# Decay differences as wide instructions, and a top-128 search over two halves side by side, in a hybrid DeltaNet / SSD / mixture-of-experts block

## The reference

```python
G = jnp.cumsum(gc, axis=-1)
decay = jnp.where(tri, jnp.exp(jnp.where(tri, G[..., :, None] - G[..., None, :], 0.0)), 0.0)
...
scores = jnp.einsum("cbgin,cbgjn->cbgij", Cc, Bc)[:, :, :, None] * decay
```

```python
aff = jax.nn.softmax(jnp.einsum("btd,de->bte", h, router_w).astype(jnp.float32), axis=-1)
gate, idx = lax.top_k(jnp.swapaxes(aff, 1, 2), cap)
xs = h[bidx, idx]
hid = jax.nn.silu(jnp.einsum("becd,edf->becf", xs, w_gate)) * jnp.einsum("becd,edf->becf", xs, w_up)
ye = jnp.einsum("becf,efd->becd", hid, w_down) * gate[..., None].astype(h.dtype)
return jnp.zeros_like(h).at[bidx, idx].add(ye)
```

## Time and profile before

| | us |
|---|---|
| median of 3 runs | 1633.59 |
| lowest, highest | 1630.49, 1635.47 |
| the profiled execution, its own time | 1629.44 |
| its span | 1627.6 |
| PE busy | 1331.3 (82%) |
| DVE busy | 864.7 (53%) |
| ACT busy | 439.4 (27%) |
| POOL busy | 214.6 (13%) |

### The profile page before, as it was taken

How to read it: one execution, slowest core, us unless ns; L and a number is a source line. 1 busy time by engine, 2 the same in 40 slices (tenths; PEclk the granted TensorE clock), 3 DMA queues, 4 the chain that set the end, 5 groups by cost and what they waited for, 6 DMA issues and landing times.

```text
span 1627.6 us, 13873 instructions
## 1 busy us (share of the span) xinstructions
PE 1331.3 (82%) x5055; PEld 774.9 (48%) x5055; DVE 864.7 (53%) x1243; ACT 439.4 (27%) x935; POOL 214.6 (13%) x190
## 2 busy tenths in 40 slices
PE   6898899999992999678788878989207999999990
PEld 1354444444452555468787774444203444444440
DVE  1257556679778466468889964555591110010115
ACT  1525524521101122244444433343101011110102
POOL 0003100210000000144444510000000110111100
PEclk9899899999995999799999998999557999999995
DMA  8204122224683000244545453332605999999936
GB/s 309 74 26 137 42 58 75 66 58 154 209 256 103 13 26 0 61 142 127 151 133 162 145 194 142 130 131 102 234 37 192 341 335 343 333 331 331 333 80 219
DMA packets 185689, 257.80 MB, mean 158 GB/s; under 512 B 48861, under 2 KB 107990, under 8 KB 185622
## 3 DMA queue, kind: packets, MB, share of 16 engines
q1 hardware_dynamic: 169078, 225.30, 41.4%
q0 software_dynamic: 7040, 25.17, 5.5%
q10 hardware_dynamic: 9504, 6.45, 1.3%
HBM read 212.38 MB, written 44.50 MB: 158 GB/s over the span
## 4 chain that ended last, share of the span: by engine, by line
PE 53%; DVE 22%; DMA 9%; ACT 8%; issue 4%; SPq 2%; POOL 0%; POOLq 0%; DVEq 0%; ACTq 0%
PE ps L1537 18%; PE ps L997 14%; PE ps L1016 6%; PE ps L352 5%; DVE arena L541 5%; DMA arena<-ada_w 3%; DMA arena<-zt_dram 2%; DVE arena L1891 2%; PE ps L962 2%; PE ps L1495 2%; DMA arena<-g_dram 2%; DVE arena L1908 1%; DVE arena L1232 1%; DVE arena L1950 1%; DVE arena L1948 1%
## 5 line engine op out<-in xcount | busy, mean ns | idle before, releaser
L1537 PE MATMUL ps<-arena 128*128 128x512 f32 (+1 forms) x1120 | 444.9, 557 | 0.0
L1537 PEld LDWEIGHTS ps<-arena 128*128 128x128 f32 x1120 | 214.2, 193 | 217.9 <-issue 212.7
L1891 DVE SCALAR_TENSOR_TENSOR arena<-arena,taps 128x1024 f32<-128x1024 f32 x160 | 227.0, 1419 | 5.7
L997 PE MATMUL ps<-arena 128*128 128x512 f32 x512 | 227.3, 597 | 1.4 <-ACT arena L1114 1.4
L352 PE MATMUL ps<-arena 128*128 128x128 f32 x1088 | 154.6, 304 | 67.5 <-ACT arena L507 48.3
L352 PEld LDWEIGHTS ps<-arena 128*128 128x128 f32 x1088 | 146.8, 216 | 78.9 <-ACT arena L507 55.1
L997 PEld LDWEIGHTS ps<-arena 128*128 128x128 f32 x512 | 96.7, 192 | 117.2 <-issue 115.2
L541 DVE SCALAR_TENSOR_TENSOR arena<-arena,G,neg_mask 128x128 f32<-128x128 f32 x208 | 121.3, 648 | 27.6 <-DMA arena<-g_dram 27.5
L1245 DVE TENSOR_TENSOR arena<-arena,ps 128x512 f32<-128x512 f32 x16 | 11.0, 687 | 225.6 <-PE ps L997 225.6
L962 PE MATMUL ps<-arena 128*128 128x512 f32 x256 | 116.2, 609 | 4.6 <-ACT arena L1062 4.6
L1016 PE MATMUL ps<-arena 128*128 128x512 f32 x256 | 112.6, 593 | 1.2 <-DVE arena L1252 1.2
(11 more groups left out here) (268 smaller groups left out, 1576.6 us busy)
## 6 DMA issues: line engine op xcount, KB each, us to landing
arena<-exp_w_gate SPq DMA_DIRECT2D x16, 2048.0 KB, 11.2
arena<-exp_w_up SPq DMA_DIRECT2D x16, 2048.0 KB, 9.0
arena<-exp_w_down SPq DMA_DIRECT2D x16, 2048.0 KB, 11.0
arena<-ada_w SPq DMA_DIRECT2D x16, 1024.0 KB, 6.2
arena<-w_in SPq DMA_DIRECT2D x28, 512.0 KB, 3.9
arena<-ada_w SPq DMA_DIRECT2D x4, 2048.0 KB, 10.5
arena<-x SPq DMA_DIRECT2D x16, 512.0 KB, 9.0
arena<-g_dram SPq DMA_DIRECT2D x16, 512.0 KB, 3.8
```

Of the source, the lines that this page charges most:

```text
L997: last = mm(ps[gu_bank[s] + j][:], xsT[s][:, k, :], ew[s][j][:, k, :], start=(k == 0), stop=(k == KD - 1))
L1537: last = mm(ps[3 * (m % 2) + gi][:, 0:w], wring[(m + 1) % NW][:, k, :], hT[:, k, o:o + w], start=(k == 0), stop=(k == KD - 1))
L1891: ins = v.scalar_tensor_tensor(accg, cin_l[ci % 2][:, j // 3:j // 3 + GR, j % 3:j % 3 + GW], tp[:, j:j + 1], accg, ALU.mult, ALU.add)
```

## The change

`diff` runs two instructions over all heads of the step, in place of one per head: the first subtracts G of the row token, read with a step of 0 along each head's 128 columns, and the second takes the minimum with the mask, read with a step of 0 over the heads. The second is linked to the first by a semaphore. So each of the 20 `diff_dn` is 2 instructions of 128x512 (before 4 of 128x128), and each of the 16 `diff_ssm` 2 of 128x1024 (before 8 of 128x128).

The search runs over 32 partitions by 512 columns: expert and half of the tokens. After 16 rounds each half has its highest 128, in descending order. One list is taken backwards; the larger of value i of the first half and value 127 - i of the second, over all i, gives the highest 128 of both. To this end the tiles of `aff` are stored by half, 4 transposes and one copy take the place of 8 and 2, and DVE has two reversed copies, one copy of 128x128 out of PSUM and 6 small instructions in place of 2.

```diff
             def diff(out, t, d, g0, n):
-                for h in range(n):
-                    last = v.scalar_tensor_tensor(out[:, h, :], out[:, h, :], G[:, t, d, g0 + h:g0 + h + 1],
-                                                  neg_mask[:, d, :], ALU.subtract, ALU.min)
-                return last
+
+                link(v.tensor_tensor(out, out, bc(G[:, t, d, g0:g0 + n], P), ALU.subtract))
+                return v.tensor_tensor(out, out, bh(neg_mask[:, d, :], n), ALU.min)
...
-        affT = take(T)[0:E_N, :]
+
+        E2, TH = 2 * E_N, T // 2
+        affT = take(TH)[0:E2, :]
...
-            for t in range(NL):
-                last = tr(ps[2 + t // 4][0:E_N, (t % 4) * P:(t % 4 + 1) * P], aff[:, t, :], ident[:])
+            for q in range(NL // 2):
+                last = tr(ps[2][0:E2, cols(q)], aff[:, 2 * q:2 * q + 2, :].rearrange("p s n -> p (s n)"), ident[:])
...
-            tr(ps[0][:, 0:E_N], topf, ident[0:E_N, 0:E_N])
-            tr(ps[0][:, E_N:2 * E_N], topv, ident[0:E_N, 0:E_N]).then_inc(sem("affps"), 1)
+            for r, src in enumerate((topv, topf, topvr, topfr)):
+                last = tr(ps[0][:, r * E2:(r + 1) * E2], src, ident[0:E2, 0:E2])
+            last.then_inc(sem("affps"), 1)
...
-            for h in range(2):
-                a(affT[:, h * 512:(h + 1) * 512], ps[2 + h][0:E_N, :], ACT.Copy).then_inc(sem("lexp"), 1)
+            a(affT, ps[2][0:E2, :], ACT.Copy).then_inc(sem("lexp"), 1)
...
-            v.tensor_copy(topf, topi).then_inc(sem("route"), 1)
+            v.tensor_copy(topf, topi)
+            v.tensor_copy(topfr, topi[:, ::-1])
+            v.tensor_copy(topvr, topv[:, ::-1]).then_inc(sem("route"), 1)
             dve.wait_ge(sem("affps"), 2)
-            v.tensor_copy(idxT, ps[0][:, 0:E_N]).then_inc(sem("route"), 1)
-            v.tensor_copy(gateT, ps[0][:, E_N:2 * E_N]).then_inc(sem("route"), 1)
+            link(v.tensor_copy(flat(two), ps[0][:, 0:4 * E2]))
+
+
+            va, ia = two[:, 0, 0:E_N], two[:, 1, 0:E_N]
+            vb, ib = two[:, 2, E_N:E2], two[:, 3, E_N:E2]
+            v.tensor_tensor(pick[:, 0], va, vb, ALU.is_ge)
+            link(v.scalar_tensor_tensor(pick[:, 1], ia, float(TH), ib, ALU.subtract, ALU.subtract))
+            link(v.tensor_tensor(pick[:, 1], pick[:, 1], pick[:, 0], ALU.mult))
+            link(v.scalar_tensor_tensor(pick[:, 1], pick[:, 1], float(TH), ib, ALU.add, ALU.add))
+            v.tensor_copy(idxT, pick[:, 1]).then_inc(sem("route"), 1)
+            v.tensor_tensor(gateT, va, vb, ALU.max).then_inc(sem("route"), 1)
```

More of the change, by code:

```diff
@@ L804, in hybrid_block @@
         sqj = take(D)
-        tk = take(3 * P)
-        topv, topf = tk[0:E_N, 0:CAP], tk[0:E_N, CAP:2 * CAP]
-        topi = take(P).bitcast(U32)[0:E_N, 0:CAP]
+        tk = take(4 * P).rearrange("p (r n) -> p r n", r=4)
+        topv, topf, topvr, topfr = (tk[0:E2, r, :] for r in range(4))
+        topi = take(P).bitcast(U32)[0:E2, 0:CAP]
+        two = take(4 * E2).rearrange("p (r n) -> p r n", r=4)
+        pick = take(2 * E_N).rearrange("p (r n) -> p r n", r=2)
         idxT = take(E_N).bitcast(U32)
@@ L1217, in dve_tail @@
                     dve.wait_ge(sem("logit"), t - 1)
-                    v.tensor_copy(aff[:, ORD[t - 2], :], ps[1][:, 0:E_N]).then_inc(sem("lcopy"), 1)
+                    o = ORD[t - 2]
+                    v.tensor_copy(aff[:, o % 4 * 2 + o // 4, :], ps[1][:, 0:E_N]).then_inc(sem("lcopy"), 1)
             dve.wait_ge(sem("lcopy"), NL)
@@ L1226, in dve_tail @@
             v.tensor_tensor(aff, aff, bc(lmax, E_N), ALU.mult).then_inc(sem("route"), 1)
-            dve.wait_ge(sem("lexp"), 3)
+            dve.wait_ge(sem("lexp"), 2)
             for r in range(CAP // 8):
```

## The result

The changed kernel takes 1562.97 us (median of 4, 1561.67 to 1565.81) against 1632.04 us for the kernel before in the same comparison: ratio 0.9587, 95% interval 0.9568 to 0.9605. Forecast was 1571 with a range of 1560 to 1592. The profiled execution has a span of 1561.5 us, 66.1 less than before.

What follows compares the result with a forecast made beforehand. The prediction took DVE's L541 in the scan, waiting for POOL, and the token search as the bounds: 36.4 + 25.0 = 61.4 us off the profiled 1629.44 gives 1568.0; allowing for the 1633.59 median, 1571, range 1560 to 1592.

Steps and rivals of the forecast that it cites:

- Reading the stage: Scan, `diff_ssm` in a long turn: two POOL instructions waited for, not five, 2.55 us less than 6.65.
- What is late next: Scan: after the change the loop over the load of `E` decides, with turns of 13.4 us.
- the short turn: Scan turn of 13.56 us before the change, with 3 POOL instructions on `diff_ssm`, taken as closed by the load of `E`.
- The estimate without the loop: Scan: a long turn less the `diff_ssm` saving and the low clock level, 12.6 us, shorter than the load loop.
- the sum: Whole kernel: 36.4 us from the scan plus 25.0 from the token search, 61.4 us less.
- The search: Token search: 25.1 us less in 47 instructions, 1.4 saved ahead, 1.5 added behind, net 25.0.
- the sum for the scan: Scan: 14 turns from 15.94 to 13.4 us and smaller terms, net 36.4 us less.
- the 1.3 set down: Scan, before the first long turn: five wide `diff_dn` at 0.26 us more each, 1.3 us lost.
- Crowded loads: Rival, scan: shorter turns stretch SP's issuing and the landing of `E`; at 1 us more, 1585 us; chance 0.18.
- POOL always first: Rival, scan: a wide instruction waits until POOL is through, turns stay near 16, 1608 us; chance 0.06.
- Slower by POOL: Rival, scan: wide instructions block POOL 2 x 1.08 us a turn and POOL closes the turn, 1640 us; chance 0.03.
- Shorter than the loop: Rival, scan: `diff_ssm` meets one POOL instruction, 3.0 us, turns of 12.5, 1557 us; chance 0.06.

Runs made afterwards that it cites:

- the repeat: The changed kernel, unchanged, measured again against the kernel before: 1563.62 us against 1629.06, ratio 0.9591.
- the scan alone: The kernel before with only the wide decay differences, token search as before: 1588.36 us against 1631.36, ratio 0.9743.
- the one profile of the old scan: The changed kernel with decay differences per head again, keeping the changed token search: 1605.14 us, ratio 0.984 to the kernel before.

## Why the prediction was right

*Reading the stage.* The step that carried it was to read the 6.65 us of L541 as 2.2 us of work and 4.5 us of waiting for POOL, and to price the wide form by how many POOL instructions it meets. The runs with one, two, four and eight instructions show it: 1.75, 3.97, 6.0, 6.65 us. Forecast for two was 3.97 to 4.13.

*What is late next.* The length of turn was right, 13.4 forecast and 13.40 measured, but not the loop behind it. The prediction read the short turn as closed by the landing of `E`. But there, too, the first instruction of `diff_dn` ended 0.15 us behind `decayed_hs` (895.58 + 0.75 and 895.14 + 1.04), and the loop over `decayed_hs` closes without the load. The forecast hit because it took the whole short turn, 13.56, and changed in it only `diff_ssm` (0.46 less forecast, 0.49 measured) and `diff_dn` (0.26 more forecast, 0.34 measured), which lie in both loops. Taken by the loop that it names, two of its terms were off and cancelled, which is luck: the load took 0.24 less (4.19 against 4.43), where the prediction had no change, and from the landing of `E` to `y_off` it was 0.57 more (2.03 against 1.46), where it had 0.26. What carried the forecast were the short turns of before: the same kernel had two lengths of turn, and the shorter one showed the next limit with durations in it. The clock went with PE's idle time before `block_vq`: at 3.18 us a long turn had a granted clock of 0.90, at 1.32 it is 1.00.

*The estimate without the loop.* 16.62 - 2.55 - 1.5 = 12.6 was too low by 0.3: without the loop the turn is 12.92. It left out that `diff_dn` grows by 0.26 and that DVE then has hardly any idle time left to hide it. It had no part in the sum.

*The search.* 25.1 predicted for the rounds, 25.0 measured; 1.5 behind them, 1.5 measured; 1.4 ahead, and from the last copy of the router's values to the first `max` 1.3 were saved. The cost forecast from the columns alone came out with the partitions doubled; the two were not varied apart.

*Where the sum missed.* 66.1 us against 61.4. Between the two profiles, 4.0 of the 4.7 lie in the merge stage, where the waits for `zt_dram` are 3.7 us shorter. That is a fact of these two profiles and not the explanation: both comparisons of the whole change, 64.5 to 70.5 us less here and 64.2 to 69.1 in the repeat, exclude 61.4, and so does the scan alone its 36.4. So the sum for the scan, or for what follows it, was some microseconds too small. Which term it was stays open: the one profile of the old scan beside the one before has turns of 16.22 in place of 15.94, which would put most of it into the turns. The first context steps cost less than the 1.3 set down, or the start varied: before the first `decay8` the executions lie between 722.9 and 727.8 us, so this can't be told.

*The rivals.* Crowded loads: from issue to use `E` took 4.2 us in the turn shown, no longer than the 4.43 before, though the window moves 162 GB/s against 143. Nor would a later landing have stretched the turn one to one: `E` came up to 0.84 us after the start of `decayed_hs` at no cost. POOL always first: out, every wide instruction had its turn after one POOL instruction. Slower by POOL: it was held up by 32 us in all, and the list of waits has nothing new for it: 5.9 us of DVE's in the context steps against 6.0 before. Shorter than the loop: out, none of the 14 latent turns is shorter than 13.39.

## What to carry to other kernels

Where two engines exclude each other as here, the price of an instruction is its own columns, plus, each time that it starts, what is left of the other engine's instruction, up to the whole of it: count starts, not columns, and merge small instructions where the other engine runs end to end, but not where it is idle. Look for turns of the same loop with different lengths; the short ones show the limit that comes next, in numbers. Before you call a load the limit, see whether the length of turn follows its landing: here it depended only on which of two engines went first. And a search of several passes over one long row was better laid over idle partitions, where the merge of the parts is a handful of small instructions.

## What the runs showed of the hardware

- A waiting instruction counts as busy on both engines. DVE's share fell from 53% to 52% and POOL's rose from 13% to 16% in a change that took 66 us off the span.
- DVE and POOL took strict turns wherever both had work waiting, in all the stretches read: they alternated one for one, whether the DVE instruction had 128, 512 or 1024 columns.
- `max`, `max_index` and `match_replace` took 1216, 1206 and 1197 ns at 1024 columns and 682, 673 and 664 at 512: if the partitions (16 and 32) don't count, 1.04 ns a column and 0.13 to 0.15 us fixed.
